# A list scheduler with measured durations that also picks ACT or VectorE for each plain evacuation, in a hybrid decoder block on eight cores

## The reference

```python
def rms_norm(x, g):
    y = x * lax.rsqrt(jnp.mean(x * x, axis=-1, keepdims=True) + 1e-6)
    return y * g

h = rms_norm(x, ln_pre_mix)                       # x (2, 8192, 1024)
z = h @ w_in + b_in
c_q, c_kv, k_r, fq, fk, fv, f_logit, ga, gb = split(z)   # 256,128,32,512,512,512,8,1024,1024
# mixer A: latent attention, 8 heads of 64 + 32 rotary
q = rms_norm(c_q, q_a_norm) @ w_uq ;  q_nope, q_rot = ... ; q_rot = rope(q_rot, positions)
c_kv = rms_norm(c_kv, kv_a_norm)
k_nope = c_kv @ w_uk ;  v = c_kv @ w_uv ;  k_rot = rope(k_r, positions)
y_mla = causal_attention([q_nope q_rot], [k_nope k_rot], v, 96 ** -0.5) @ w_o_mla
# mixer B: forgetting attention, 8 heads of 64
F = cumsum(log_sigmoid(f_logit))
y_fox = causal_attention(fq, fk, fv, 64 ** -0.5, bias=F_t - F_s) @ w_o_fox
merged = sigmoid(ga) * y_mla + sigmoid(gb) * y_fox
x = x + rms_norm(merged @ w_out, ln_post_mix)
h2 = rms_norm(x, ln_pre_mlp)
m = square(relu(h2 @ w_ff1)) @ w_ff2              # 4096 wide
out = x + rms_norm(m, ln_post_mlp)
```

## Time and profile before

| | us |
|---|---|
| median of 3 runs | 2247.06 |
| lowest, highest | 2243.12, 2332.93 |
| the profiled execution | 2245.74 |
| its span, slowest core | 2244.2 |
| spans of the 8 cores | 2227.7 to 2244.2 |
| mean granted TensorE clock, by core | 0.978 to 0.983 |

### The profile page before, as it was taken

One profiled execution on the slowest core, in us unless ns is written; L12 is line 12 of the kernel. 1 busy time (PEld: TensorE's weight loads), 2 busy tenths in 40 slices (PEclk: granted clock), 3 DMA queues, 4 the chain that ended last, 5 costly groups with the idle time before them and its releaser, 6 DMA issues.

```text
span 2244.2 us, 39297 instructions; the slowest of 8 cores (2227.7 to 2244.2 us)
## 1 busy us (share of the span) xinstructions
PE 2092.5 (93%) x11810; PEld 1031.1 (46%) x11810; DVE 702.0 (31%) x1355; ACT 1481.1 (66%) x2186; POOL 326.2 (15%) x416
## 2 busy tenths in 40 slices
PE   3797998999999999999999999898999999999997
PEld 2354555455555455554443344444444444444443
DVE  2565655234444234333110002523231351111101
ACT  2665765797788898778899997777689341312121
POOL 3311300012000011000000002121120231222221
PEclk9899999999999999999999999999999999999999
DMA  7675886357755465443334979786746344020201
GB/s 158 164 211 154 220 191 163 105 142 171 184 143 142 107 146 151 124 121 91 98 97 125 199 163 201 186 198 162 198 120 169 93 141 169 29 75 20 76 1 57
DMA packets 164609, 306.48 MB, mean 137 GB/s; under 512 B 40603, under 2 KB 98870, under 8 KB 161462
## 3 DMA queue, kind: packets, MB, share of 16 engines
q1 hardware_dynamic: 154400, 273.50, 44.0%
q0 software_dynamic: 8800, 29.84, 8.5%
q10 hardware_dynamic: 1206, 0.63, 0.2%
HBM read 254.11 MB, written 88.01 MB: 152 GB/s over the span
## 4 chain that ended last, share of the span: by engine, by line
PE 83%; ACT 5%; DMA 4%; issue 3%; DVE 3%; POOL 1%; ACTq 0%; SPq 0%; DVEq 0%; POOLq 0%
PE sp L598 20%; PE oa L625 18%; PE sp L1417 6%; PE yb L1088 5%; PE sp L1483 4%; PE yb L896 4%; PE yb L888 4%; PE oa L1483 2%; ACT PT L609 2%; PE yb L1331 2%; PE yb L1483 2%; PE oa L1417 2%; PE yb L1417 2%; DMA rc<-ropec 2%; PE yb L1349 1%
## 5 line engine op out<-in xcount | busy, mean ns | idle before, releaser
L609 ACT ACTIVATE PT<-sp 128x1024 bf16<-128x1024 f32 (+1 forms) x1088 | 1029.5, 985 | 216.3 <-PE sp L598 120.0
L598 PE MATMUL sp<-QQ,KT 96*128 96x512 bf16 (+20 forms) x2560 | 648.9, 340 | 39.4 <-ACT PT L609 30.6
L625 PE MATMUL oa<-PT,VV 128*65 128x512 bf16 (+13 forms) x2560 | 637.3, 341 | 0.3 <-ACT PT L609 0.3
L598 PEld LDWEIGHTS sp<-QQ,KT 96*128 96x128 bf16 (+1 forms) x2560 | 204.3, 98 | 321.3 <-issue 222.6
L625 PEld LDWEIGHTS oa<-PT,VV 128*65 128x65 bf16 x2560 | 253.4, 112 | 205.2 <-issue 5.3
L1417 PE MATMUL sp<-h2T,wff 128*128 128x512 bf16 x640 | 142.2, 379 | 0.1
L1088 PE MATMUL yb<-hTo,wG 128*128 128x512 bf16 x512 | 135.9, 390 | 5.1 <-DVE eg L1092 4.1
L1092 DVE TENSOR_SCALAR eg<-yb,colb 128x512 f32<-128x512 f32 x64 | 47.8, 749 | 207.9 <-PE oa L625 82.7
L896 PE MATMUL yb<-wfv,hT 128*128 128x512 bf16 x432 | 107.6, 387 | 4.5 <-DVE kst L473 1.8
L605 PE MATMUL sp<-maskTs,ident 128*128 128x64 bf16 (+1 forms) x576 | 109.6, 190 | 0.0
L1420 ACT ACTIVATE rl<-sp 128x512 bf16<-128x512 f32 x80 | 47.6, 595 | 89.0 <-PE sp L1417 67.4
(11 more groups left out here) (311 smaller groups left out, 2405.2 us busy)
## 6 DMA issues: line engine op xcount, KB each, us to landing
xt<-xb SPq DMA_DIRECT2D x64, 512.0 KB
VV<-Vm SPq DMA_DIRECT2D x40, 520.0 KB
VV<-Vf SPq DMA_DIRECT2D x40, 520.0 KB
KT<-KTm SPq DMA_DIRECT2D x80, 256.0 KB
KT<-KTf SPq DMA_DIRECT2D x80, 256.0 KB
KT<-KR SPq DMA_DIRECT2D x80, 128.0 KB
Vf<-vst SPq DMA_DIRECT2D x16, 520.0 KB
Vm<-vmst SPq DMA_DIRECT2D x16, 520.0 KB
```

Of the source, the lines that this page charges most:

```text
L598: P.op("pe", lambda e: e.matmul(SP[sp][:, bi * 512 + off:bi * 512 + off + N], lhsT=KT[0:dk, ks, (kb % 16) * 128:(kb % 16 + 1) * 128], rhs= ...
L609: P.op("act", lambda e: e.activation(out=PT[:, pt_, 0:tot], in_=SP[sp][:, 0:tot], func=AF.Exp, scale=scale), st[0:len(grp)], [pttok], n=tot)
L625: P.op("pe", lambda e: e.matmul(OA[a][0:65, c0:c0 + N], lhsT=VV[:, vs, vo:vo + 65], rhs=PT[:, pt_, off:off + N], start=st_, stop=sp_), [pt ...
```

## The change

Three things. Planned durations change: ACT n/1.2 + 140 ns, VectorE n/0.96 + 155 ns; squares with a sum are planned at 1250, 480 and 360 columns instead of 1024, 256 and 128, and a 1024-column copy on VectorE at 512. A plain evacuation is now recorded for VectorE with an alternative on ACT, and `_list_schedule` enters it in both ready lists; it goes to the engine whose planned start is earlier, where ACT's start is counted later by a bias: 0 ns for work recorded before attention, 300, 500 and 700 ns for that merged with blocks 0, 1 and 2, 1500 ns for block 3, 0 behind it. The shares are gone. `MASKV` only moves to another line.

```diff
-ACT_SHARE = (0.7, 0.4, 0.2, 0.1)
+ACT_BIAS = (0.0, 300.0, 500.0, 700.0, 1500.0, 0.0)
...
     if eng == "act":
-        return n / 1.2 + 100.0
+        return n / 1.2 + 140.0
     if eng == "dve":
-        return n / 0.96 + 90.0
+        return n / 0.96 + 155.0
...
-    def _add(self, eng, fn, reads, writes, dma, cow=(), track=True, n=None):
+    def _add(self, eng, fn, reads, writes, dma, cow=(), track=True, n=None, alt=None, lo=0.0):
         i = Ins(eng, _snap(fn), dma)
         i.idx = len(self.ins)
-        i.cost = _cost(eng, dma, n)
+        i.cost = max(_cost(eng, dma, n), lo)
+        if alt is not None:
+            i.alt = (alt[0], _snap(alt[1]), _cost(alt[0], False, alt[2]), alt[3])
...
+        def enter(k):
+            ready[ops[k].eng].append(k)
+            stale.add(ops[k].eng)
+            if ops[k].alt is not None:
+                ready[ops[k].alt[0]].append(k)
+                stale.add(ops[k].alt[0])
...
+                    if ops[k].alt is not None and ops[k].alt[0] == e:
+                        st += ops[k].alt[3]
                     if cand is None or (st, k) < cand:
                         cand = (st, k)
...
+            if i.alt is not None:
+                a = i.alt
+                o = a[0] if e == i.eng else i.eng
+                ready[o].remove(k)
+                stale.add(o)
+                if e == a[0]:
+                    i.eng, i.fn, i.cost = a[0], a[1], a[2]
+                    st -= a[3]
+                i.alt = None
...
         def evac_copy(out_ap, in_ap, reads, writes, eng=None, cow=(), n=512):
-            if eng is None:
-                act_acc[0] += act_share[0]
-                eng = "act" if act_acc[0] >= 1.0 else "dve"
-                if eng == "act":
-                    act_acc[0] -= 1.0
+            nd = n // 2 if n == 1024 else n
+            fa = lambda e: e.activation(out=out_ap, in_=in_ap, func=AF.Copy)
+            fd = lambda e: e.tensor_copy(out=out_ap, in_=in_ap)
             if eng == "act":
-                P.op("act", lambda e: e.activation(out=out_ap, in_=in_ap, func=AF.Copy), reads, writes, cow, n=n)
+                P.op("act", fa, reads, writes, cow, n=n)
             else:
-                P.op("dve", lambda e: e.tensor_copy(out=out_ap, in_=in_ap), reads, writes, cow, n=n)
+                P.op("dve", fd, reads, writes, cow, n=nd, alt=("act", fa, n, ACT_BIAS[act_phase[0]]))
```

More of the change, by code:

```diff
@@ L19 @@
 DFF = 4096
-MASKV = -3.0e5
 RESCHED_SEGS = (0, 1)
@@ L23 @@
 PH_END = (0, 0.92, 0.95, 0.97)
-ACT_SHARE = (0.7, 0.4, 0.2, 0.1)
+ACT_BIAS = (0.0, 300.0, 500.0, 700.0, 1500.0, 0.0)
+MASKV = -3.0e5
 PI = float(np.pi)
@@ L73 @@
 class Ins:
-    __slots__ = ("eng", "fn", "idx", "deps", "sig", "signo", "dma", "dsem", "dval", "dprev", "cost", "seg", "bar", "nosig", "nb")
+    __slots__ = ("eng", "fn", "idx", "deps", "sig", "signo", "dma", "dsem", "dval", "dprev", "cost", "seg", "bar", "nosig", "nb", "alt")
     def __init__(self, eng, fn, dma):
@@ L84, in __init__ @@
         self.nb = 0
+        self.alt = None
         self.deps = []
@@ L137, in _add, with op @@
         return i
-    def op(self, eng, fn, reads=(), writes=(), cow=(), track=True, n=None):
-        return self._add(eng, fn, reads, writes, False, cow, track, n)
+    def op(self, eng, fn, reads=(), writes=(), cow=(), track=True, n=None, alt=None, lo=0.0):
+        return self._add(eng, fn, reads, writes, False, cow, track, n, alt, lo)
     def dma(self, q, fn, reads=(), writes=(), cow=()):
@@ L174, in _list_schedule @@
         ready = {e: [] for e in self.ENGS}
+        def enter(k):
[4 more added lines that the diff above has]
+                stale.add(ops[k].alt[0])
+        stale = set(self.ENGS)
         for k, i in enumerate(ops):
             if indeg[k] == 0:
-                ready[i.eng].append(k)
+                enter(k)
         eng_free = {e: 0.0 for e in self.ENGS}
@@ L181, in _list_schedule @@
         best = {}
-        stale = set(self.ENGS)
         order = []
@@ L215, in _list_schedule @@
                     pick = c
+                    pe_ = e
             st, k = pick
             i = ops[k]
-            e = i.eng
+            e = pe_
             ready[e].remove(k)
             stale.add(e)
+            if i.alt is not None:
[7 more added lines that the diff above has]
+                i.alt = None
             if i.dma:
@@ L248, in _list_schedule @@
                     depready[u] = dr
-                    ready[w.eng].append(u)
-                    stale.add(w.eng)
+                    enter(u)
         self.sim_end = max(fin) if fin else 0.0
@@ L869, in evac_bias @@
         def evac_bias(out_ap, in_ap, b_ap, reads, writes):
-            act_acc[0] += act_share[0]
-            if act_acc[0] >= 1.0:
-                act_acc[0] -= 1.0
-                P.op("act", lambda e: e.activation(out=out_ap, in_=in_ap, func=AF.Identity, bias=b_ap), reads, writes)
-            else:
-                P.op("dve", lambda e: e.tensor_scalar(out=out_ap, in0=in_ap, scalar1=b_ap, scalar2=None, op0=ALU.add), reads, writes)
+            fa = lambda e: e.activation(out=out_ap, in_=in_ap, func=AF.Identity, bias=b_ap)
+            P.op("dve", lambda e: e.tensor_scalar(out=out_ap, in0=in_ap, scalar1=b_ap, scalar2=None, op0=ALU.add), reads, writes,
+                 alt=("act", fa, 560, ACT_BIAS[act_phase[0]]))
         def chunk_slots(p):
@@ L1217, in build_program @@
         for k in range(1, 4):
-            act_share[0] = ACT_SHARE[k]
+            act_phase[0] = k
             piece_lim[0] = first_of[k]
@@ L1223, in build_program @@
             merge(x_steps(k - 1), yl[marks[k - 1]:(marks[k] if k < 3 else len(yl))], end=PH_END[k], after_y=open_next)
-        act_share[0] = 0.0
+        act_phase[0] = 4
         emit_pref(pref2, 100)
@@ L1405, in build_program @@
         aft2 = soft_after()
-        act_share[0] = 0.5
+        act_phase[0] = 5
         y_post = y_own + [ybank(OA[k], 0, oa_toks[k]) for k in range(2)]
```

11 lines of the change are left out of this document (5 added, 6 removed).

## The result

The change takes 2211.9 us (median of 4 runs) against 2246.2 us for the kernel before, measured beside it (median of 4). The ratio is 0.9848, with a 95% interval of 0.9827 to 0.9869: 34 us, 1.5%. The forecast was 2235, so the sign was right and the gain three times the forecast 10.5 us. The profiled execution of the change took 2212.6 us; its slowest core is core 6 (2211.0 us), where core 3 was the slowest before (2244.2 us). (Some executions, with the change and without, were disturbed, with the cores of one die slower at a lower granted clock, and are left out of all ratios.)

What follows compares the result with a forecast made beforehand. TensorE was busy 93% of the span, so only its idle time and late-starting matmuls could be won. Terms 0 - 4 - 3.5 - 3 + 0 = -10.5 us from 2245.7 gave 2235 us; range 2208 to 2261.

Steps and rivals of the forecast that it cites:

- the cut of one run: After 1120 us: 32 output matmuls in a row become 16, 6 and 10 with attention between, worth up to 4.92 us.
- 0 to 80 us (0): Start: gains of 1.1 and 0.7 us against up to 1.8 us lost to two more ACT table swaps; bounds -2, +3.
- 80 to 211 us (-4): Projections before attention: 3 us from evacuations that may change engine, 1 us from better order; bounds -12, +3.
- rival (a): Waits are hidden anyway or only change names: 2246 us, chance 0.25.
- 211 to 1120 us (-3.5): Attention with projections: half of 11.1 us of PE waits for ACT saved, VectorE waits up 2 us; bounds -11, +5.
- Both signs to look for: From 211 to 1120 us: PE's waits for exponentials near 5 us, for VectorE near 16 us.
- Its sentence that matmuls fill that stretch: Argument against ACT's relief counting in full: matmuls, not ACT, fill the stretch from 211 to 1120 us.
- 1120 to 1752 us (-3): Last 512 queries' attention with output projections: only the order moves, one run of output matmuls is cut; bounds -10, +6.
- Behind 1752 us (0): Feed-forward: two more h2st evacuations on ACT, among waits of a few us; no gain, bounds -1, +1.
- (b): VectorE becomes the late one: one in three of 45 moved copies delays PE, 10 us plus 3: 2259 us, chance 0.15.
- (c): All 28 us taken off ACT between 211 and 1120 us count, plus 4 + 5 elsewhere: 2209 us, chance 0.13.
- (d): VectorE's flush rule holds: each moved copy takes 1.11 us instead of 0.69, 19 us more: 2254 us, chance 0.02.

Runs made afterwards that it cites:

- e1: The kernel before with all the new planned durations, engine shares kept (124 evacuations on ACT): 2211.6 us, ratio 0.9850.
- e2: The change with the old planned durations, so the engine choice alone (81 evacuations on ACT): 2247.4 us, ratio 1.0017.
- the families: Kernels grouped by planned durations: all old (four orders, mean ratio to the kernel before 0.9987) and all new (seven orders, mean 0.9871).
- e5: The kernel before with only VectorE's planned constant raised, 90 to 155 ns: 2240.7 us, ratio 0.9990.
- e7: The kernel before with only the planned column numbers of single forms changed (squares, 1024-column VectorE copy, ACT's biased evacuation): 2231.2 us, ratio 0.9943.
- e9: The kernel before, ACT results planned to reach their users 40 ns later, ACT itself free as before: 2235.1 us, ratio 0.9945.
- e12: The kernel before with all ACT instructions except the exponentials planned 40 ns longer: 2235.8 us, ratio 0.9966.
- e13: The kernel before with only the norm statistic's two ACT steps planned as traced (Ln 293 ns, Exp 202 ns): 2236.7 us, ratio 0.9957.
- e15: The kernel before with the planned latency between engines at 176 instead of 170 ns, a meaningless shake: 2236.5 us, ratio 0.9947.
- e17: The kernel before with the planned latency between engines at 164 instead of 170 ns, a meaningless shake: 2240.1 us, ratio 0.9985.
- e10: The kernel before, each ACT instruction planned to occupy ACT 40 ns longer, results on time as before: two usable runs, 2237.8 and 2238.1 us, no ratio.
- e11: The kernel before with only the 1088 exponentials planned 40 ns longer: 2237.8 us, ratio 0.9971.
- e3: The change with every evacuation choice in the four attention blocks made for VectorE (64 on ACT): 2219.9 us, ratio 0.9882.
- e8: The kernel before with all new planned durations, constants raised further to ACT + 180 and VectorE + 220 ns: 2224.4 us, ratio 0.9922.

## Why the prediction was right or wrong

**The split of the gain between the two halves of the change: wrong.** The prediction costed evacuations that change engine and gave the order itself 1 us (in 80 to 211 us) and the cut of one run. e1 and e2 show the reverse: durations and their order 33 us, choice no gain (within the half per cent that one order has by luck).

**0 to 80 us (0): right in its parts, and it came to nothing.** The two more table loads are there. The timeline of the change has six between 47 and 68 us, that of before four between 50 and 70; the two new ones are that for `fl` at 49.85 and that for `cso` at 57.36:

```profile
47.91 1.28 ACT L885 ACT_TABLE_LOAD   x1 [1.72 <-DVE eg L884]
...
49.85 1.28 ACT L943 ACT_TABLE_LOAD   x1
...
57.36 1.28 ACT L1154 ACT_TABLE_LOAD   x1
...
60.40 1.28 ACT L478 ACT_TABLE_LOAD   x1
```

PE's idle time in 0 to 80 us fell on the page's cores from 49.2 to 42.9 us, but the first exponential starts 1.3 us later than before, mean of the cores, for both terms up to it together (-4 forecast).

**80 to 211 us (-4): wrong.** PE's idle time there is 22.9 us, not near 17 (before 20.6). The waits changed their names, as rival (a) said: summed over the view, PE stands 18.9 us for VectorE (before 16.7) and 4.0 us for ACT (before 3.4). The first rows of PE's waits in that stretch of the change:

```profile
PE yb L1090 <- DVE qb L1084: 2.7, 2, 2.5
PE yb L1008 <- DVE vst L913: 1.7, 2, 1.0
PE oa L911 <- ACT kst L888: 1.5, 1, 1.5
PE yb L911 <- DVE kst L487: 1.5, 2, 1.0
```

**211 to 1120 us (-3.5): the step that failed.** The same work, exponentials 0 to 624, fell by 24.7 us. The term was made of ACT's relief against VectorE's load alone and put the new order in this stretch at nothing, without a reason. By the families that order is what counts there: exponentials 0 to 624 take 978 to 985 us with the old durations and 960 to 968 with the new, 16.8 us between the means; the other 8 of the 24.7 are, by that estimate, this pair's luck. Both signs to look for failed. PE's waits in 211 to 1120 us of the change:

```profile
PE sp L616 <- ACT PT L627: 8.5, 12, 2.1
PE yb L1103 <- DVE eg L1107: 3.9, 5, 1.1
```

The exponentials stand at 8.5 us and not near 5 (9.1 before), so ACT's relief did not reach PE. PE's waits for VectorE went *down*, 14.6 to 9.1 us, where 16 were forecast, although VectorE carries 27 us more. ACT's busy time fell by 20 us between exponentials 0 and 624 (mean of the cores) and by 16 on the whole page, not by 28: the two added table loads give back 2.6, and priced at their own length instructions count too high, since neighbours overlap (1088 exponentials of 984 ns are 1071 us, the page has them busy for 1030). By e1 and e2, what decides is where the instructions stand in the lists, which the prediction read only for the three places it showed.

Its sentence that matmuls fill that stretch was wrong too. Of the 24.7 us, PE's idle time gives 10.3 (33.4 to 23.0, mean of the cores), its busy time 14.3. A part of that is the granted clock: the length of each stretch times what the clock lacks of 1 is 10.9 us before and 3.2 us in the change, nearly 8 us less. What makes up the rest of the busy time was not traced. The deepest place, ahead of exponential 624, in the windows view of before and then of the change:

```profile
1090.00:1100.00 10.00, 10.00 (x48) 4.56 (x47) 2.25 (x3) 9.82 (x11) 0.00 (x0) 1.00 0.30 75
1100.00:1110.00 10.00, 7.96 (x25) 2.60 (x24) 0.00 (x0) 8.18 (x9) 0.00 (x0) 0.74 0.63 194
1110.00:1120.00 10.00, 9.98 (x43) 4.28 (x42) 1.58 (x3) 5.96 (x7) 0.00 (x0) 0.92 0.00 0
```

```profile
1070.00:1080.00 10.00, 9.90 (x45) 4.09 (x44) 1.50 (x2) 10.00 (x12) 0.00 (x0) 1.00 0.40 75
1080.00:1090.00 10.00, 7.84 (x28) 3.01 (x27) 0.75 (x1) 7.11 (x8) 0.00 (x0) 0.83 0.44 166
1090.00:1100.00 10.00, 10.00 (x48) 4.59 (x47) 1.60 (x3) 8.58 (x10) 0.00 (x0) 1.00 0.17 50
```

In the timeline of before, PE went from its usual pace (7 matmuls of 512 columns in 1.67 us) through waits for exponentials to 11 of the same matmuls in 4.33 us (the view ends at 1112):

```profile
1092.88 1.67 PE L1088 MATMUL yb<-hTo,wG 128*128 128x512 bf16 x7
...
1102.58 0.59 PE L598 MATMUL sp<-QQ,KT 70*128 70x512 bf16 x2 [0.83 <-ACT PT L609]
...
1104.53 0.74 PE L598 MATMUL sp<-QQ,KT 70*128 70x512 bf16 x2 [0.92 <-ACT PT L609]
...
1108.05 4.33 PE L1088 MATMUL yb<-hTo,wG 128*128 128x512 bf16 x11
```

For most of these TensorE had the lower of its two levels, 1.2 GHz. Much the same two waits for exponentials stand in the change, but what the clock lacks comes to 3.4 us before (0.26 and 0.08 of 10 us each) and to 1.7 us in the change (0.17): the lower level lasted twice as long. Why it came back sooner was not tried.

**1120 to 1752 us (-3): right in its reason, half of the size.** Exponentials 700 to 800, where the run of 32 stands, take 107.1 us before and 103.4 in the change. In every kernel run here that keeps the run whole (before, e2, e5, e7, e9, e12, e13, e15, e17) it is 106.4 us or more, in every one that cuts it 103.1 to 104.2: 3.7 us for 3 forecast. All of exponentials 624 to 1087 gave 5.9, though; most of the other 2 us stands in exponentials 950 to 1087, where the prediction named no cause. The cut comes with the planned time that ACT is taken by exponentials (e10 and e11 have it, e9 and e12 not). PE's idle time in the fixed window is 32.7 us for 31 forecast. Only this term was of the order alone, and only it was traced to its cause ahead of time.

**Behind 1752 us (0): off by 3.4 us**, 492.0 to 488.6 behind the last exponential. It comes with the durations (e1 488.7, e2 491.2). Here PE's transposes of `h2n`, ahead of the feed-forward, stand for VectorE 4.1 us before and 2.4 in the change, mean of the cores.

**The rivals.** (a) *Hidden anyway* fits the engine choice (e2). (b) *VectorE late* would have shown in e3, with 60 evacuations more on VectorE than e1: 8 us slower than e1, no more than a shake of the order gives, and PE's waits for VectorE don't show it. e2's start, 8.2 us late, may be a case of it; what held it was not tried. (c) *ACT's relief in full* gave the nearest time (2209) for a cause that the runs refute: e1 has no relief. (d) *The flush*, all of it met by PE, would have made e2 slower by 43 x 0.42 = 18 us; it measures 4. The rows decide it: before, the instruction behind a 128x512 copy of 0.68 us starts as early as 0.60 us after the copy's start. The Trainium skill ("VectorE: DVE Perf Modes", "The DRAIN you can't avoid") says in the same paragraph that an instruction which is not held starts earlier than the flush allows, which the prediction left out; the trace agrees with that part.

**What stays open.** Why orders planned with the new durations are better. The nearest theory was that planned ACT chains that are too short put waiting instructions ahead of ready ones. For it: VectorE waits less for statistics before exponential 80 (43.8 us before, 33.1 in the change, 32.0 in e1, means of the cores), and e13, which mends only that chain, shortens exponentials 40 to 80 by 6.0 of 13.4 us. Against it: the old plan itself holds the waits around 348 us nearly as traced. A shake by 6 ns, with all old durations, shortens the same stretch by 8.6 us and has none of the waits for `ckr` either (e17), though it gives 2.6 of it back in the 40 exponentials before. And VectorE's idle time ahead of the norm product does not follow the time: 34.1 us in the change, 44.9 in e1, which is as fast, 41.8 in e9, which is 23 us slower. So the theory is argued, not shown, and has no measured share of the 1.2%. What no run tells apart is whether the new durations help because they are true, or because this scheduler happens to make better orders with dearer instructions; e8 was meant to and lies within luck.

## What to carry to other kernels

Change a list scheduler's duration table and its rules apart, and run each alone, before either is credited: here the table had all of the gain that shows and the rule none. Before crediting a reordering of under about half a per cent, shake the order with a change that means nothing and see how far the time moves by itself. When a wait is put to one engine, look what stands ahead in that engine's list and whom that waited for: it may be a third. And before such a wait is blamed on a plan that did not know the chip, look whether the plan already holds it.
